# ScalarE's order in the memory stages: the next block's high part ahead of the copy of the block's second bank

## The reference

```python
def memory_cross_attention(h, m, wq, wkv, wo):      # m: 256 x 1024, wkv: 1024 x 2048
    q = (h @ wq).reshape(b, t, XA_HEADS, XA_HEAD_DIM)
    k, v = jnp.split(m @ wkv, 2, axis=-1)
    ...
    s = jnp.einsum("bthd,bmhd->bhtm", q, k).astype(jnp.float32) * (XA_HEAD_DIM ** -0.5)
    p = jax.nn.softmax(s, axis=-1).astype(v.dtype)
    o = jnp.einsum("bhtm,bmhd->bthd", p, v).reshape(b, t, D_MODEL)
    return o @ wo
```

## Time and profile before

| what | value |
|---|---|
| median of 3 runs | 2449.25 us (2448.51 to 2450.19) |
| the profiled execution | 2448.76 us, its span 2446.9 us |
| TensorE busy | 2401.6 us, 98% of the span |
| ScalarE, GpSimd, VectorE busy | 960.6, 999.1, 1233.6 us |
| granted TensorE clock | 0.998 of full speed |

### The profile page before, as it was taken

How to read it: one execution, slowest core, us unless ns; L and a number is a source line. 1 busy time by engine, 2 the same in 40 slices (tenths; PEclk the granted TensorE clock), 3 DMA queues, 4 the chain that set the end, 5 groups by cost and what they waited for, 6 DMA issues and landing times.

```text
span 2446.9 us, 30098 instructions
## 1 busy us (share of the span) xinstructions
PE 2401.6 (98%) x11174; PEld 1902.9 (78%) x11174; DVE 1233.6 (50%) x2086; ACT 960.6 (39%) x1453; POOL 999.1 (41%) x744
## 2 busy tenths in 40 slices
PE   8999999999999999999999999999899999999998
PEld 6777668977888887858878888887557977888887
DVE  4453545334333436694356545555764334555545
ACT  3354345433322226524444222226766433322223
POOL 4323224233454445535515454454022333454443
PEclk9999999999999999999999999999999999999999
DMA  5212213421322223223222322322102421323231
GB/s 170 87 53 83 85 44 117 155 86 52 125 91 98 92 97 104 87 69 103 69 73 87 104 90 99 103 86 67 35 18 86 155 86 52 104 88 102 87 102 69
DMA packets 176732, 217.86 MB, mean 89 GB/s; under 512 B 6568, under 2 KB 157658, under 8 KB 176614
## 3 DMA queue, kind: packets, MB, share of 16 engines
q1 hardware_dynamic: 175302, 214.06, 27.0%
q10 hardware_dynamic: 1312, 2.21, 0.3%
HBM read 214.14 MB, written 2.12 MB: 88 GB/s over the span
## 4 chain that ended last, share of the span: by engine, by line
PE 90%; DVE 4%; ACT 3%; issue 1%; POOL 1%; DMA 1%; SPq 0%; DVEq 0%; ACTq 0%
PE ps_l L800 77%; PE ps_l L1035 3%; PE ps_l L926 2%; PE ps_s L1085 2%; PE ps_l L1160 1%; PE ps_s L1143 1%; ACT w_hi L1369 1%; POOL w_lo L649 1%; PE ps_s L1223 1%; PE ps_s L1238 1%; PE ps_s L1050 1%; DVE arena L1968 0%; DVE small L2673 0%; DVE x_T L2284 0%; DVE a_lo L1974 0%
## 5 line engine op out<-in xcount | busy, mean ns | idle before, releaser
L649 POOL TENSOR_TENSOR w_lo<-w_raw,w_hi 128x512 fp32r<-128x512 f32 (+1 forms) x740 | 998.9, 1381 | 1421.6 <-ACT w_hi L1369 1401.6
L800 PE MATMUL ps_l<-a_hi,w_hi 128*128 128x512 f32 x1936 | 764.1, 395 | 2.2 <-POOL w_lo L649 2.1
L800 PE MATMUL ps_l<-a_lo,w_hi 128*128 128x512 f32 x1952 | 758.6, 389 | 0.0
L800 PE MATMUL ps_l<-a_hi,w_lo 128*128 128x512 f32 x1936 | 754.1, 390 | 0.0
L1369 ACT ACTIVATE w_hi<-w_raw 128x2048 fp32r<-128x2048 f32 (+2 forms) x196 | 370.6, 1891 | 570.4 <-PE ps_l L800 553.1
L800 PEld LDWEIGHTS ps_l<-a_hi,w_hi 128*128 128x128 f32 x1936 | 363.2, 188 | 87.6 <-issue 7.7
L800 PEld LDWEIGHTS ps_l<-a_lo,w_hi 128*128 128x128 f32 x1952 | 366.0, 188 | 77.8 <-issue 3.3
L800 PEld LDWEIGHTS ps_l<-a_hi,w_lo 128*128 128x128 f32 x1936 | 362.8, 187 | 77.2
L800 PE MATMUL ps_l<-b_hi,w_hi 128*128 128x512 f32 (+1 forms) x908 | 335.5, 370 | 7.8 <-POOL w_lo L649 3.3
L800 PE MATMUL ps_l<-b_lo,w_hi 128*128 128x512 f32 (+1 forms) x908 | 333.0, 367 | 0.0
L800 PE MATMUL ps_l<-b_hi,w_lo 128*128 128x512 f32 (+1 forms) x908 | 333.0, 367 | 0.0
(11 more groups left out here) (276 smaller groups left out, 2638.1 us busy)
## 6 DMA issues: line engine op xcount, KB each, us to landing
w_raw<-in_ffn_w_up_dram SPq DMA_DIRECT2D x44, 1024.0 KB, 5.0
w_raw<-in_w_dram SPq DMA_DIRECT2D x32, 1024.0 KB, 5.2
w_raw<-in_ffn_w_down_dram SPq DMA_DIRECT2D x22, 1024.0 KB, 4.9
w_raw<-in_w_in_dram SPq DMA_DIRECT2D x20, 1024.0 KB, 5.3
w_raw<-in_xa_wkv_dram SPq DMA_DIRECT2D x16, 1024.0 KB, 5.6
w_raw<-in_w_kv_mem_dram SPq DMA_DIRECT2D x8, 1024.0 KB, 5.6
w_raw<-in_xa_wq_dram SPq DMA_DIRECT2D x8, 1024.0 KB, 5.1
w_raw<-in_xa_wo_dram SPq DMA_DIRECT2D x8, 1024.0 KB, 5.1
```

The source lines that it names most:

```text
L649: e.tensor_tensor(w_lo[:, b % 2, o], w_raw[:, b % 2, o], w_hi[:, b % 2, o].bitcast(F32), ALU.subtract).then_inc(w_lo_made[by], 1)
L800: ins = pe.matmul(o, *((v, w) if swap else (w, v)), start=first and n == 0, stop=last and n == 2)
```

## The change

In both functions the call of hi moves ahead of the copy of the block's last group, behind the wait for that group. No instruction is added or removed, and all semaphores count as before.

```diff
@@ block_copies
                     for q in range(per):
                         wait_group(act, L, g + per * j + q)
+                        if q == per - 1:
+                            hi(b + j + 2)
                         act.activation(dst(per * j + q), bank(L, g + per * j + q)[:, 0:cols], ACT.Copy)\
                             .then_inc(l_free["a"], 1)
-                    hi(b + j + 2)
@@ key_copies
                 for q in (0, 1):
                     g = L.base[f"xk{c}"] + 2 * j + q
                     wait_group(act, L, g)
+                    if q:
+                        hi(plan.block_base[f"xk{c}"] + j + 2)
                     act.activation(kT[:, 2 * j + q, :], bank(L, g)[:, 0:MEM], ACT.Copy).then_inc(l_free["a"], 1)
-                hi(plan.block_base[f"xk{c}"] + j + 2)
```

## The result

The changed kernel takes 2455.73 us (median of 12 runs, 2452.47 to 2457.27), the kernel before 2449.48 us beside it (12 runs, 2447.77 to 2453.58). The ratio is 1.0022, with an interval of 1.0014 to 1.0030: slower by 0.2%, or 6.2 us. The forecast was 2451.3 us (+2.1 us), and the measured median lies 2.0 us above the upper end of its range, 2453.7. The profiled execution took 2455.69 us, its span 2453.9 us.

What follows compares the result with a forecast made beforehand. TensorE, busy 98% of the span, was taken as the bound. Keys -0.6 us plus second-stage value blocks +2.7 us gave +2.1 us, so 2449.25 + 2.1 = 2451.3 us, range 2448.6 to 2453.7 us.

Steps and rivals of the forecast that it cites:

- Nothing behind gives the 2.7 back: After value block 3, second stage: TensorE runs 32.92 us without a break, so the 2.7 us delay stays in full.
- The value blocks' term: Second memory stage: the last copy waits behind a load and high part, so pc_out_b starts late; +2.7 us.
- About 3.2 us: Predicted sign: TensorE's gap before pc_out_b grows from 0.8 to about 3.2 us, released by the last copy.
- The keys' term: Second memory stage's keys: earlier high parts let GpSimd's pieces and VectorE's additions end earlier before the norm; -0.6 us.
- is the same sum in another order: Second stage's keys: ScalarE's own work up to the next square stays equal in total, only reordered.
- The first and third stage: First and third memory stages, twice 8 blocks: earlier high parts don't reach TensorE, which has 1.2 us to spare; 0.
- The port rival: First and third stages: VectorE's earlier low part blocks GpSimd's piece through SBUF sharing; 2455.9 us, chance 0.04.
- Rival 1: Before pc_out_b: TensorE waits for GpSimd's second piece, not the last copy; -0.9 us, 2448.3 us, chance 0.09.
- Rival 2: First and third stages: VectorE's low part holds up GpSimd's piece; 4.6 on top of 2.1, 2455.9 us, chance 0.04.
- Rival 3: Later stretches give the value-block delay back and the keys' gain is lost in turns with GpSimd; 2449.3 us, chance 0.11.
- The chance of 0.06: Whole kernel slower than 2454.1 us: 0.04 from the SBUF port case plus 0.02 for the main case's upper tail.
- the worst of both terms: Whole kernel: keys at +1.3 and second-stage value blocks at +3.9 together, summing to +5.2 us.

Runs made afterwards that it cites:

- One spare copy: Kernel before, old order, plus one 128x1024 in-place copy on ScalarE ahead of the last copy of value block 3, second cross-attention: 2452.61 us, +1.9.

## Why the prediction was wrong

**The step that failed** is "Nothing behind gives the 2.7 back: TensorE runs on for 32.92 us". It took the length of the stage behind the gap from a row at full clock. The gap that the same sum made 2.7 us longer brought 1.2 GHz behind it, and the stage took 35.72 us (35.48 and 35.76 in the repeats). No term stood for it, no rival either, and the clock of 0.998 over the whole span hid that it is lost in single stretches. The Trainium skill, "TensorE: Matmul & The Clock Gate", section "HAM oscillation — how this bites in real kernels", warns of just this: a wait that leaves TensorE idle long enough has it throttled, and the next work starts cold. These runs agree, by the gaps of 3.7 to 4.1 us; they also show falls behind gaps of 1.8 to 2.2 us, in some executions and not in others.

With the slow matmuls the terms come to -0.4 + 2.75 + 2.8 = +5.2 us (stretches A and B). The last 1.0 of the 6.2 us stays open: stretch C varies by more than that.

**The value blocks' term** was right as a mechanism, and in size: counted from the start of stretch B, pc_out_b starts 41.72 us on instead of 38.97, +2.75, and the run with TensorE kept busy measured stretch B at +2.8 with all of the waits left in. Its releaser, the four claims, the load's time and the release of 0.35 us all came as worked out. "About 3.2 us" for the gap was too short: the sum's own parts are 0.78 and 2.7, and value block 3 ends earlier (0.20 us measured, 0.3 in the bounds but left out of the gap); 0.78 + 2.75 + 0.20 is the 3.73 that came.

**The keys' term** was -0.6 and measured -0.4 (stretch A is 364.85 to 364.87 in all eight profiles with the new order there). The first high part gained only 0.2 us of the 0.36: the row after has 962.81, which is 0.06 behind the copy's end, where I let it start 0.10 ahead. GpSimd's second run started 0.46 earlier, and the last addition before the norm ended 0.45 earlier, at 976.55 instead of 977.00, now in 1.08 us and not 1.34. But ScalarE's square ended only 0.18 earlier, at 976.57, and is now the last that the norm waits for: the releaser changed from VectorE to ScalarE, and the wait only shrank from 1.8 to 1.6 us. The remark that ScalarE's own work "is the same sum in another order" was right, and it was the bound that the term left out: even an addition 0.6 us earlier would, by these rows, have gained about 0.4.

**The first and third stage** were 0 as far as the profiles can tell: from the row of 48 matmuls at 411.22 to the MLP's start it is 204.2 to 204.7 us in the fourteen profiles, with either order, and from the row at 1880.26 to the last FFN 204.23 before and 204.15 after. The port rival did not happen (5.04 us for the four pieces).

**Rival 1** fell: with the copy late, TensorE waited 3.73 us for it. **Rival 2** has about the right time, 2455.9, for a cause that is not there. **Rival 3** fell too: nothing was given back. The chance of 0.06 for slower by over 0.2% was far too low: what I took for the worst of both terms left out the term that doubled the larger one.

Left open: what decides the stretches at half clock that come by execution. One spare copy cost 1.1 us in stretch B, yet the medians differ by 1.9; its profile also has a fall in stretch A (366.97, +1.7), with the order of before there. Such a fall, behind the gap of 1.8 us before the norm, is in 2 of the 6 profiles with the old order of the keys, and in none of the 8 with the new one, where the gap is 1.6 us. The stretch near 1795 was slow in 6 of 8 profiles of kernels that were delayed before pc_out_b by 1 us or more, and in 2 of the 6 others. Both are too few to tell.

## What to carry to other kernels

Before a wait is put ahead of a copy on an in-order engine, look who claims the buffer that the copy frees; a claim of all banks at once turns a late copy of one into a stall of all. When a change makes a gap in TensorE's row longer, price the gap twice, as idle time and as work behind it at half clock. Take from the rows how often the clock column falls behind gaps of that length: here behind every one of 3.7 to 4.1 us, and behind those of 1.8 to 2.2 us in some executions. And a move that helps in one place and harms in another, as here, should be made block by block: what decides is whether the load or the last group comes later, and whether anyone waits for the bank by then.

## What the runs showed of the hardware

Idle gaps of 0.8 to 1.9 us before pc_out_b left the granted clock at 1.00, and so did one of 3.0 us in its one profile. Gaps of 3.7 to 4.1 us brought a stretch at 0.50 in all five profiles that have one. Elsewhere shorter gaps did so in some executions and not in others of the same kernel: 2.0 us near 1795 and 2.1 to 2.2 us near 1667; 1.8 us before the norm behind the keys did in two of the six profiles that have this gap. So the length of the gap alone does not say whether the clock falls. The cost of one fall behind the gaps of 3.7 to 4.1 us was 1.6 to 2.8 us. Fifteen matmuls without use, 3.6 us of TensorE's time in a gap that was there anyway, kept the clock at 1.00 behind it and made the changed kernel 3.7 us faster by the medians, 2.8 us of it in stretch B.
